# Prompt attention: the row maxima of both score maps by one VectorE instruction instead of two

## What is computed

```python
s = jnp.einsum('bqhmd,bkhmd->bhmqk', qi, k).astype(F32) * scale      # m = 2 maps
s = jnp.where(kpos[None, :] <= qpos[:, None], s, -jnp.inf)
pr = jax.nn.softmax(s, axis=-1)
att = pr[:, :, 0] - lam * pr[:, :, 1]
return jnp.einsum('bhqk,bkhe->bqhe', att.astype(v.dtype), v)
```

## Time and profile before

| | |
|---|---|
| median of 3 runs | 4073.3 us (4068.99 to 4077.49) |
| profiled execution | 4074.64 us, of which the span from first to last instruction is 4072.9 us |
| mean granted TensorE clock | 0.922 |
| PE busy | 3537.0 us (87%) |
| DVE busy | 1379.2 us (34%) |
| ACT busy | 807.4 us (20%) |
| the attention stage | from about 398 to 614 us of the span |

### The profile page before, as it was taken

One profiled execution on the slowest core, in us unless ns is written; L12 is line 12 of the kernel. 1 busy time (PEld: TensorE's weight loads), 2 busy tenths in 40 slices (PEclk: granted clock), 3 DMA queues, 4 the chain that ended last, 5 costly groups with the idle time before them and its releaser, 6 DMA issues. The chain is left out here.

```text
span 4072.9 us, 66731 instructions
## 1 busy us (share of the span) xinstructions
PE 3537.0 (87%) x29134; PEld 2934.8 (72%) x29134; DVE 1379.2 (34%) x1966; ACT 807.4 (20%) x1428; POOL 523.6 (13%) x354
## 2 busy tenths in 40 slices
PE   5997884979999999699974499997877799999996
PEld 3665452669999999366532399997534499999995
DVE  1199546141111111400039644332373221111113
ACT  1000332031111111100125332332020121211111
POOL 0000210012212221000014311110000012222220
PEclk8998996989999999799986699998678899999998
DMA  1122531011111110122215412110110111111111
GB/s 74 52 41 95 166 125 54 30 42 38 53 46 39 55 47 27 42 73 73 73 40 200 151 43 55 43 43 16 44 36 32 36 37 47 43 51 42 42 50 56
DMA packets 192507, 239.68 MB, mean 59 GB/s; under 512 B 122323, under 2 KB 141524, under 8 KB 191220
## 3 DMA queue, kind: packets, MB, share of 16 engines
q1 hardware_dynamic: 183668, 205.99, 17.0%
q0 software_dynamic: 5120, 16.78, 1.2%
q10 hardware_dynamic: 3456, 12.98, 0.8%
HBM read 189.51 MB, written 46.20 MB: 58 GB/s over the span
## 5 line engine op out<-in xcount | busy, mean ns | idle before, releaser
L2457 PE MATMUL f_out<-f_u_hi,f_weights_hi 128*128 128x352 f32 x2112 | 685.5, 325 | 58.1 <-DVE f_u_lo L2499 58.1
L2458 PE MATMUL f_out<-f_u_lo,f_weights_hi 128*128 128x352 f32 x2112 | 680.5, 322 | 0.0
L2459 PE MATMUL f_out<-f_u_hi,f_weights_lo 128*128 128x352 f32 x2112 | 679.7, 322 | 0.0
L2433 POOL TENSOR_TENSOR f_weights_lo<-f_weights,f_weights_hi 128x1024 fp32r<-128x1024 f32 (+2 forms) x168 | 323.5, 1926 | 1932.6 <-ACT f_weights_hi L2469 1932.6
L2457 PEld LDWEIGHTS f_out<-f_u_hi,f_weights_hi 128*128 128x128 f32 x2112 | 399.3, 189 | 60.3 <-issue 48.8
L2458 PEld LDWEIGHTS f_out<-f_u_lo,f_weights_hi 128*128 128x128 f32 x2112 | 399.8, 189 | 0.0
L2459 PEld LDWEIGHTS f_out<-f_u_hi,f_weights_lo 128*128 128x128 f32 x2112 | 398.7, 189 | 0.0
L1230 PE MATMUL mp_out<-mp_mixed,mp_weights 128*128 128x352 f32 x1152 | 344.6, 462 | 41.5 <-DVE mp_mixed L1203 40.5
L2522 DVE TENSOR_TENSOR f_product<-f_out,f_gate 128x352 f32<-128x352 f32 x132 | 69.3, 525 | 882.7 <-PE f_out L2459 882.7
L2457 PE MATMUL f_out<-f_inner_hi,f_weights_hi 128*128 128x352 f32 x1056 | 341.4, 323 | 4.0 <-DVE f_inner_lo L2530 4.0
L1230 PEld LDWEIGHTS mp_out<-mp_mixed,mp_weights 128*128 128x128 f32 x1152 | 220.2, 191 | 165.9 <-issue 45.7
(11 more groups left out here) (359 smaller groups left out, 4986.1 us busy)
## 6 DMA issues: line engine op xcount, KB each, us to landing
f_weights<-in_w_gu SPq DMA_DIRECT2D x88, 512.0 KB, 3.7
scratch_rkv<-mp_out_tile ACTq DMA_DIRECT2D x24, 528.0 KB, 5.3
pc_rkv<-scratch_rkv SPq DMA_DIRECT2D x24, 528.0 KB, 6.3
f_weights<-in_w_down SPq DMA_DIRECT2D x48, 256.0 KB, 2.6
mp_weights<-in_w_rkv SPq DMA_DIRECT2D x24, 512.0 KB, 4.5
f_weights<-in_w_down SPq DMA_DIRECT2D x32, 320.0 KB, 2.9
all_hT<-in_x SPq DMA_DIRECT2D x2, 4224.0 KB, 13.1
all_hT<-in_cache_k SPq DMA_DIRECT2D x32, 256.0 KB, 4.9
```

What stands on the lines that cost most here:

```text
L2433: pool.tensor_tensor(lo[:, s, :w], raw[:, s, :w], hi[:, s, :w].bitcast(F32), ALU.subtract).then_inc(lo_ready, 1)
L2457: pe.matmul(out, hi[:, s, w], x_hi, start=(k == 0), stop=False)
L2458: pe.matmul(out, hi[:, s, w], x_lo, start=False, stop=False)
L2459: last = pe.matmul(out, lo[:, s, w], x_hi, start=False, stop=(k == parts - 1))
```

## The change

The two PSUM regions become one of 2048 columns (four banks), of which S[0] and S[1] are the halves. The two reductions of a unit become one, over both halves at once with two results for each row; it waits for `scored0` and `scored1`, and raises a single `maxed`. Both exps wait for that.

```diff
-        S = [st.bank(f"scores{m}", 1024) for m in range(2)]
+        both = st.bank("scores", 2048)
+        S = [both[:, m * 1024:(m + 1) * 1024] for m in range(2)]
...
-        scored, maxed, exped = ([st.sem(f"{n}{m}") for m in range(2)] for n in ("scored", "maxed", "exped"))
+        scored, exped = ([st.sem(f"{n}{m}") for m in range(2)] for n in ("scored", "exped"))
+        maxed = st.sem("maxed")
...
                     for m in range(2):
                         dve.wait_ge(scored[m], u + 1)
-                        dve.tensor_reduce(nmax[:, u % 2, m:m + 1], S[m][:, :(i + 1) * P], AXX, ALU.max,
-                                          negate=True).then_inc(maxed[m], 1)
+                    dve.tensor_reduce(nmax[:, u % 2], both[:].rearrange("p (m k) -> p m k", m=2)[:, :, :(i + 1) * P], AXX,
+                                      ALU.max, negate=True).then_inc(maxed, 1)
...
                     for m in range(2):
-                        act.wait_ge(maxed[m], u + 1)
+                        act.wait_ge(maxed, u + 1)
```

## The result

The changed kernel takes 4085.7 us (median of 10 runs, 4076.56 to 4091.82) against 4072.64 us for the kernel before (10 runs, 4067.13 to 4083.48): a ratio of 1.0030 with a 95% interval of 1.0018 to 1.0041, or 12.2 us more (7.3 to 16.7); the medians lie 13.1 us apart. The forecast was 8.4 us more. The profiled execution took 4091.82 us, the slowest of the ten, with a span of 4090.1 us against 4072.9.

What follows compares the result with a forecast made beforehand. The stage was taken as bound by a chain going round the engines once per unit; 5.4 us of waits plus 3.0 us of clock falls made 8.4 us over the 4073.3 us median, about 4082 us; range 4074 to 4089.

Steps and rivals of the forecast that it cites:

- Which units wait for what: In the stage's 32 units, the copy comes last with room in 24; the second reduction ends after the first exp's start in 8.
- The instruction's length: The merged reduction on DVE takes 2.29 us for 2048 columns, at most 2.36 us plus a 0.25 us margin.
- The rival of the four banks: Each merged reduction on DVE takes 0.25 us more than the line: 2.5 us over the forecast, 4084 us; chance 0.03.
- The waits, 5.4 us: The first exp starts later in seven units, mostly i = 7 and i = 6, and unit 0: 5.4 us in sum.
- That the count of operations is worth something: Rival: 32 fewer DVE instructions save 0.07 us in each of 32 units, 2.2 us, giving 4071 us; chance 0.02.
- The clock, 3.0 us: how many falls: Two of the four lengthened TensorE pauses (i = 7) bring a fall from 2.4 to 1.2 GHz, 1.5 us each: 3.0 us.
- The clock: the price of a microsecond at the low level: A microsecond with TensorE's clock at 1.2 GHz costs 0.44 us; a fall, 3.4 us low, costs 1.5 us.
- unit 9's pause: TensorE's pause in unit 9 lengthens by 1.2 us, lowering its work from 2.62 to about 1.4 of 4.00 us.
- at most one further fall: Rival: same 5.4 us delay, but the lengthened TensorE pauses bring no clock fall or one: 4078.7 to 4080.2 us; chance 0.43.

## Why the prediction was right

Its range held the time and its sign was right; the sum, 8.4 us, lies inside the measured interval of 7.3 to 16.7. By its steps:

- *Which units wait for what.* Right in all but one. Seven waits of ACT for the maxima appeared where they were forecast, beside the one at the start, and unit 27 has none, as forecast. The reading that the copy comes last with room in 24 units was wrong for unit 29 (i = 5): in the kernel before, its second reduction (589.64 to 591.46) already ends 0.04 us after the first exp's start (591.42). Its exp now waits 0.20 us. The experiment with one instruction in 24 units left a head at 46.49 us.
- *The instruction's length.* Right to 0.01 us, from a line through one-map reductions and a neighbour with 32 results. The rival of the four banks is out by this, and by the run with the region alone.
- *The waits, 5.4 us.* Right in size: 5.6 (standard error 0.5) by the fit, 1.7 against 1.6 us in the head that can be seen without a fall. Unit by unit in the changed kernel's trace, the first exp stands 0.3 to 1.4 us later behind the copy's end than before; that sums to 6.3 us, and unit 19's 0.5 of it is taken up by PE as forecast. The 0.10 us from the second mask's end to the start of an instruction with two waits was not in the sum.
- *That the count of operations is worth something.* The rival fell: DVE's saved instructions lay beside other work, with the extra matmuls and without. The overlap of 0.08 us that the prediction holds against the reason for the rule is in the trace, but the section of the Trainium skill that it names (The DRAIN you can't avoid, of VectorE: DVE Perf Modes) says itself that a next operation which is not held starts earlier, so the overlap does not contradict that page.
- *The clock, 3.0 us: how many falls.* The mechanism was right: the changed kernel has more falls, and extra matmuls in the pauses took falls away, and time with them. The size is the least certain part of the sum. In the trace the count came out too low. Six falls were forecast in place of four, and there are eight: the four lengthened pauses had been taken at one in two and all four were followed by a fall, and a further one came behind a unit of i = 6 (unit 11, where PE waits 1.79 us for the exps instead of 1.30), which was left out. Five of the eight last twice as long as a fall of before. That makes 32 us more at the low level, where two falls would be 6.8. But the traced execution is the slowest of ten. The granted clock over the whole span, on record for every execution, has a mean of 0.9194 for the changed kernel, and of 0.9202 to 0.9209 for the kernel before on the three chips of the experiments. That is 8 to 15 us more at the low level, with a standard error of some 4, or 3 to 5 us of time at 0.35. Of the measured 12.2 us, 5.6 are the waits; the 6.6 that remain carry the measurement's own uncertainty of nearly 5. So how far the 3.0 was too small on the median stays open.
- *The clock: the price of a microsecond at the low level.* The 0.44 us of the prediction holds in the two comparisons of single stretches (0.43 and 0.44). In the changed kernel it is too high: 32 x 0.44 us and the waits would come to 20 us, and the stage grew by 17.2. There the two seem to overlap in part, which no run separates.

One estimate on the way to the clock was wrong. The prediction had unit 9's pause come down to about 1.4 of 4.00 us of work, less than ahead of any fall of before. The window ahead of the fall holds 2.46 us, where it was 2.62 without a fall, and the fall begins at 463.4, when the 1.26 us of waiting for the exps are still to come. So the fall in unit 9 came true on a wrong estimate, which is partly luck. That the clock depends on the work in it is shown by the run with extra matmuls, in which the same late exp brought no fall.

The rival "at most one further fall" had 0.43. The four further falls of the trace and the 8 to 15 us of the ten executions, against 3.4 us for one fall, both speak against it.

## What to carry to other kernels

Two instructions on one engine are not two costs when the second lies under the consumer of the first. Before merging them, look in the timeline for the consumer that starts between their ends; it will start after the merged one, and what it feeds moves with it. Where the loop holds TensorE, count the pause too: a microsecond of waiting can cost a second one through the granted clock, and matmuls of no use in a pause can win time. They have to lie in a pause: where TensorE had none, three of them cost 1.3 us.

## What the runs showed of the hardware

- A reduction over two halves of a region of four PSUM banks, with two results, took 2.292 us for 2048 columns, 1.047 ns for a column and one fixed part, as one over a single map.
- Extra work on TensorE made the kernel faster: ten matmul instructions of 256 columns in one pause of unit 9 took 2.32 us, and the scores behind it fell from 1.22 to 0.70 us. In the kernel before, the matmuls that took away all four falls of the traced execution made the stage 4.7 us shorter and the program 6.1 and 6.7 us faster by the medians of two runs.
- The same program fell to the low level for 16 us of this stage in one execution and, with only its two PSUM regions made one, for 34 us in another; the stage took 7.2 us longer. The scatter of the runs (4064 to 4084 us for the kernel before over all chips) is of the same kind of size; that it comes from there was not traced run by run, and the rest of the program varies by as much: outside the stage the twelve profiles take 3858.8 to 3869.2 us.
